# Storing an input-GEMM tile as one transfer of 576 KB instead of three of 192 KB

## What is computed

```python
def _layer(x, att_cache, ml_state, conv_buf, s5_state, p):
    h = _rmsnorm(x, g)
    (aq, ak, av, az, mq, mk, mv, mo, mz, mif, cb, cc, cx, cz, su, sz) = _split(h @ w_in)
    ya = band_attention(aq, ak, av, rel_bias)            # own chunk and 8 before it
    ym = sigmoid(mo) * mlstm(mq, mk, mv, mif, ml_state)
    yc = cb * conv3(cc * cx)
    ys = s5(su, ...)                                      # state space, GELU, GLU
    y = concatenate([silu(z) * yb for yb, z in ((ya, az), (ym, mz), (yc, cz), (ys, sz))])
    return x + y @ w_out
```

## Time and profile before

| | us |
|---|---|
| median of 3 runs | 2525.08 |
| lowest and highest of them | 2524.63, 2527.05 |
| the profiled execution | 2520.97 |
| its span, first to last instruction | 2519.2 |
| TensorE's mean granted clock in it | 0.969 of full |

### The profile page before, as it was taken

The page is one execution under the profiler, slowest core; times in us unless marked ns, Lnnn a source line. Parts: engine busy times, 40 slices in busy tenths (PEclk is TensorE's granted clock), DMA queues, the critical chain, the costliest instruction groups (busy, mean ns, idle before and its releaser), DMA issues.

```text
span 2519.2 us, 36324 instructions
## 1 busy us (share of the span) xinstructions
PE 2375.7 (94%) x14397; PEld 2179.6 (87%) x14397; DVE 753.8 (30%) x1225; ACT 479.5 (19%) x794; POOL 504.5 (20%) x292
## 2 busy tenths in 40 slices
PE   5999999999999999899999999999999765999997
PEld 4999999989999999899998898989999544888886
DVE  7220000022222221111163643531122355353433
ACT  6110000112222222122201011010110102343321
POOL 1222222222222222122222221212121340000000
PEclk8999999999999999999999999999999877999999
DMA  5121212432323231333232221322232648455562
GB/s 200 54 70 61 71 60 78 147 110 102 120 95 126 89 132 65 131 122 119 105 106 81 81 89 57 114 90 68 95 99 82 211 145 299 139 194 199 192 221 83
DMA packets 149949, 296.13 MB, mean 118 GB/s; under 512 B 26080, under 2 KB 89036, under 8 KB 146016
## 3 DMA queue, kind: packets, MB, share of 16 engines
q1 hardware_dynamic: 141792, 278.54, 32.4%
q10 hardware_dynamic: 8064, 16.25, 1.9%
HBM read 234.91 MB, written 78.70 MB: 124 GB/s over the span
## 4 chain that ended last, share of the span: by engine, by line
PE 86%; DVE 6%; DMA 5%; issue 1%; SPq 1%; ACT 1%; DVEq 0%; ACTq 0%; POOLq 0%
PE G L801 20%; PE G L803 19%; PE G L802 19%; PE X L1131 3%; PE X L1132 3%; PE X L1133 3%; PE G L1131 2%; PE G L1132 2%; PE G L1133 2%; PE X L1004 1%; PE X L983 1%; PE X L893 1%; PE X L886 1%; PE X L855 1%; PE X L998 1%
## 5 line engine op out<-in xcount | busy, mean ns | idle before, releaser
L801 PE MATMUL G<-hhi,whi 128*128 128x384 f32 x2928 | 1006.7, 344 | 8.1 <-issue 6.2
L802 PE MATMUL G<-hlo,whi 128*128 128x384 f32 x2928 | 985.2, 336 | 0.0
L803 PE MATMUL G<-hhi,wlo 128*128 128x384 f32 x2928 | 985.2, 336 | 0.0
L801 PEld LDWEIGHTS G<-hhi,whi 128*128 128x128 f32 x2928 | 554.2, 189 | 34.1 <-issue 24.6
L802 PEld LDWEIGHTS G<-hlo,whi 128*128 128x128 f32 x2928 | 554.6, 189 | 1.1
L803 PEld LDWEIGHTS G<-hhi,wlo 128*128 128x128 f32 x2928 | 553.7, 189 | 0.0
L773 POOL CAST whi<-wr 128x1024 fp32r<-128x1024 f32 x122 | 137.2, 1125 | 1473.9 <-PE G L803 1338.4
L775 POOL TENSOR_TENSOR wlo<-wr,whi 128x1024 fp32r<-128x1024 f32 x122 | 307.3, 2519 | 9.8
L1148 ACT ACTIVATE ev<-G 128x384 f32<-128x384 f32 x183 | 89.7, 490 | 871.6 <-PE G L803 871.3
L1852 DVE TENSOR_TENSOR olo<-orw,ohi 128x1024 fp32r<-128x1024 f32 x96 | 112.2, 1221 | 176.0 <-ACT ohi L1344 175.8
L1344 ACT ACTIVATE ohi<-orw 128x1024 fp32r<-128x1024 f32 x96 | 95.4, 1050 | 203.5 <-DMA orw<-w_out_t 74.3
(11 more groups left out here) (366 smaller groups left out, 2024.4 us busy)
## 6 DMA issues: line engine op xcount, KB each, us to landing
wr<-w_in_t SPq DMA_DIRECT2D x122, 512.0 KB, 4.5
orw<-w_out_t SPq DMA_DIRECT2D x96, 512.0 KB, 5.0
u_scratch<-ev SPq DMA_DIRECT2D x183, 192.0 KB, 1.9
xin<-x_all SPq DMA_DIRECT2D x9, 1024.0 KB, 4.8
cv<-u_scratch SPq DMA_DIRECT2D x16, 576.0 KB, 7.5
yr<-y_scratch SPq DMA_DIRECT2D x12, 768.0 KB, 9.0
xo<-x_all SPq DMA_DIRECT2D x3, 3072.0 KB, 12.4
y_all<-fo SPq DMA_DIRECT2D x9, 1024.0 KB, 4.0
```

Source lines behind the costliest of these rows:

```text
L801: mm(G[:, j, 0:GC], whi[:, kh, k], hhi[:, kk, hs], start=(kk == 0), stop=False)
L802: mm(G[:, j, 0:GC], whi[:, kh, k], hlo[:, kk, hs], start=False, stop=False)
L803: last = mm(G[:, j, 0:GC], wlo[:, kh, k], hhi[:, kk, hs], start=False, stop=(kk == 15))
```

## The change

The three stores of a tile become one. `store_u` is called once for a tile, where the store of bank 2 was; it waits for the evacuation of bank 2 (the count 3T + 6 covers all three banks) and sends the whole row of 1152 columns, 4608 B for each partition, where a bank's row had 1536 B. The three semaphores `u_stored[j]` become one. ScalarE's evacuation of any bank of tile T waits until the whole tile T - 1 has landed, where it waited for its own bank alone; `stored` waits once in place of three times. Bytes, buffers and the order on the engines are otherwise the same.

```diff
-        u_stored = [sem(f"u_stored{j}") for j in range(3)]
+        u_stored = sem("u_stored")
...
-            def store_u(T, j):
-
-                sp.wait_ge(evac_done, 3 * T + j + 4)
-                sp.dma_start(uT[T, :, GC * j:GC * j + GC], ev[:, j]).then_inc(u_stored[j], 16)
+            def store_u(T):
+
+                sp.wait_ge(evac_done, 3 * T + 6)
+                sp.dma_start(uT[T], ev[:, :, :].rearrange("p j n -> p (j n)")).then_inc(u_stored, 16)
 
             def gemm(T, kh, j, more=True):
                 if j == 0 and more:
                     load_w(T + 1, kh)
-                if kh == 1:
-                    store_u(T, j)
+                if kh == 1 and j == 2:
+                    store_u(T)
 
             def stored(T):
 
-                for j in range(3):
-                    sp.wait_ge(u_stored[j], 16 * T + 32)
+                sp.wait_ge(u_stored, 16 * T + 32)
...
             def evac(T, kh, j, func, scale=1.0):
                 if kh == 1:
                     act.wait_ge(bank_full, 3 * T + j + 4)
-                    act.wait_ge(u_stored[j], 16 * T + 16)
+                    act.wait_ge(u_stored, 16 * T + 16)
```

More of the change, by code:

```diff
@@ L730, in _ @@
             for s, n in ((xt_mm, 16), (h_done, 4), (w_split, 2), (half0_mm, 1), (bank_full, 3), (evac_done, 3),
-                         (u_stored[0], 16), (u_stored[1], 16), (u_stored[2], 16), (s_mm, 1), (s_add, 1),
+                         (u_stored, 16), (s_mm, 1), (s_add, 1),
                          (tp_mm, 1), (tp_evac, 1), (y_done, 1), (ay_stored, 16), (kt_mm, 4), (so_mm, 3), (sy_done, 1),
```

## The result

The median of six runs of the kernel after is 2534.02 us (2530.70 to 2537.69), against 2523.99 us for six runs of the kernel before: 1.0039 times the time, 95% interval 1.0028 to 1.0050. The change costs some 10 us; the forecast was 2528.0 us, from 2523.5 to 2532.0. A second set of runs of the same two kernels gave 1.0029 (1.0018 to 1.0039), some 7 us. So the direction that the sum had was right (+2.9 us), the size was less than half of what was measured, and "within 0.2%", which had most of the chances, was wrong.

The account below looks back on a forecast made before the run. The prediction took TensorE's matmuls as the bound (busy 94% of the span); removed issues were worth 0, and stage-end delays of 0.93 + 0.93 + 0.15 + 0.93, some 2.9 us, on a 2525.08 us median gave 2528.0 us, range 2523.5 to 2532.0.

Parts of the forecast that it names:

- A: Stage end at 486 us, tile 16: last store, K and V copies and `az` load all start later; +0.93 us, bounds 0 to 0.95.
- Rival 4: Whole kernel: 122 fewer transfers save their fixed parts; under 2520.0 us; chance 0.03 for faster by over 5 us.
- Rival 1: Hidden: the engines make good the burst at A, B and D; 0 to 1.5 us, some 2525.8 us; chance 0.24.
- B: Stage end at 1002 us, tile 32: `az` store queued behind the last store delays the sample stage's loads; +0.93 us.
- D: Stage end at 1687 us, tile 52: GELU and S5 state stores land later, delaying the first mLSTM load; +0.93 us.
- C: Stage end at 1260 us, tile 40: gaps between four `sz` stores absorb most extra bytes; +0.15 us, bounds 0 to 0.93.
- E: Stage end at 1965 us, tile 60: room for the extra bytes, so `gl` load starts unchanged; 0, bounds 0 to 0.93.
- rival 3: Behind C: longer TensorE idle time drops its clock to half, costing 1.5 to 3 us; some 2530.5 us; chance 0.12.
- Rival 2: Ends of S5 groups 0 to 2: burst delays TensorE's instruction loads, 3 x 0.93 = 2.8 us more; 2530.8 us; chance 0.08.

Follow-up runs that it names:

- e4_after_pad16: The kernel after with 16 small transfers added to SP's queue in the dense stage, ahead of the convolution's first state store; 1.0022 times the kernel before.
- e5_before_table_late: The kernel before with one redundant VectorE memset in each S5 group, so that VectorE's power table is made later; 1.0029 times the kernel before.

## Why the prediction was wrong

**The frame held.** TensorE is the bound, the dense stage kept its pace, the 122 removed issues are worth nothing (0.9992 with 56 tiles merged), a 576 KB store took 2.73 us at A where 2.78 was read for it, and TensorE was busy all of the 350 us of the dense stage, so it waited for no evacuation. Rival 4, faster by the fixed part of each transfer, is ruled out. The Trainium skill, DMA: Bandwidth & Descriptors, section Anatomy of one DMA — SWDGE (gpsimd) path, has a fixed cost of some 2.0 us a transfer; the estimate made from it, 244 us for 122 transfers one after the other, shows nowhere in the runs. Rival 1, hidden, is ruled out at B and D, and at A on the mean.

**B and D were right.** Over all twenty traces B's idle time is 8.69 to 8.98 us (nine) with tile 32 in three stores and 9.61 to 10.72 (eleven) with it in one, 1.2 more on the mean; D's is 2.13 to 2.82 us (nine) with tile 52 in three stores and 3.15 to 3.51 (eleven) with it in one, 0.9 more. The forecast was 0.93 for each.

**Three terms failed: A was too small, and what C and E set off was put at nothing.** No one of them carries the miss: the runs have 1.6 to 3.5 us at A in place of 0.93, 1.3 behind C in place of 0, and some 1.5 behind E in place of 0.

**A: "the two queues share to the end, and a later start of one stays a later end".** I priced the delay of SP's eight copies and of `az` at its own length, 0.93, and gave it 0.95 as its upper bound. The rows show that the copies that start later also lose share, and that SP takes 0.8 us longer to issue them. A's idle time over the traces that can be compared (ScalarE's issue at 0.8 us, copies in their place, no hold):

| tile 16 leaves in | idle time at A, us | mean |
|---|---|---|
| three stores | 6.02, 8.33, 9.43, 6.53, 6.55, 6.86 | 7.3 |
| one store | 10.22, 9.95, 8.37, 7.71, 9.08, 8.10, 8.64 | 8.9 |

That is 1.6 us on the mean (by the scatter in the two rows between 0.1 and 3.0, so the table alone would not rule out 0.93); the single-end runs, on one chip, gave 3.5 us of time for 2.9 of idle time. I put it between 1.6 and 3.5, against 0.93 with a bound at 0.95. The row that should have warned me was on the table: `az` took 17.60 us for 512 KB, where the stretch at B moves 428 GB/s, so its time was made by its neighbours and not by its bytes.

**C: "passes on what there is"; rival 3 had the right place with the wrong start.** The idle time itself went from 2.08 to 2.46 us on the mean of ten traces each, 0.38 where I had 0.15. What I didn't see is what hangs on it: VectorE's table, half a microsecond ahead of GpSimd's cast. Four executions in ten pay 3.1 to 3.5 us for that, 1.3 on the average over them. Rival 3 priced a fall of the clock behind C at 1.5 to 3 us and blamed the idle time at C; the clock there stayed full even behind 2.86 us of idle time (`e4_after_pad16`, 1.00 from 1282 to 1297 us), and fell behind the new wait of 1.49 us. (My reading of the bytes at C was loose too: the slices from 1258.95 to 1259.85 have a mean of 290 GB/s, which is not full beside 428.)

**E: "finds the store landed".** The load of `gl`, which I had looked at, cost nothing that can be told from scatter: its first matmul comes 22.3 to 24.0 us behind the last projection tile with tile 60 in three stores, 23.2 to 23.9 in the five traces of after. (The 0.34 MB that I read there are 0.30 by the row; that changes nothing.) But the stretch behind tile 60 is longer with one store on every chip that has both kinds, 1.5 us on the average, where I had 0, and in the first pair of traces 4.8 of the 5.9 us arise between 2010 and 2070 us of before, where the convolution begins, behind the loads with which my reading of E ended.

**Rival 2.** The wait for instructions at the first group end was 2.24 us before and 2.16 after; a second pair of traces had 2.10 and 2.45. There is no 0.93 per end.

**The sum, as it should have been:** A 1.6 to 3.5, B 1.2, C 0.4 and 1.3, D 0.9, the tail 1.5, together 6.9 to 8.8 us, against 10.0 and 7.3 us measured in two sets of runs. Without A the sum is 5.3, and the two kernels with later copies differ by 5.7 (4.3 by the ratios). The parts of the tail and of A are averages over traces that scatter by more than their size, and how a store at tile 60 delays the convolution is open.

The range failed for one reason: I had bounded each stage's cost by the bytes' own time, and added nothing for what meets what in the stages behind. The chance of 0.17 for "slower by over 0.2%" was put on rivals at two places, while the sum of four delays already stood at 2.9 of the 5 us that were needed. That the direction came out right is owed to B and D above all, where the mechanism held.

## What to carry to other kernels

Merging transfers could have paid only where someone waits for their fixed part, and here nobody does; where they end a stage, the last bytes leave later, and the stage end pays for them. A delay is worth its own length only if nothing else starts at that moment: where another queue's large copies or another engine's operation begin within a microsecond, ask which comes first now and what it costs to come second. Take a second trace of the kernel before, too: two of them differed by 7.7 us, more than twice the forecast. Here the copies on ScalarE's queue were worth as much as the change: issued later, they made the kernel before 8 us faster by the ratio (0.9967) and 10 by the medians.

## What the runs showed of the hardware

- A 512 KB load took 7.9 and 8.6 us with the other queue empty and 16.3 to 21.3 beside two copies of 1984 KB on it. How the two queues share depends on which starts first: with eight 320 KB copies on SP's queue starting 0.9 us later, the first 1984 KB copy on ScalarE's queue landed in 12.4 to 14.3 us in place of 15.4 to 17.1, and the eight copies in 12.8 to 13.2 (median of eight) in place of 11.2 to 12.0 (seven traces against six).
- A VectorE operation of 0.42 us (128x256, two inputs) that starts behind a GpSimd operation took 1.15 to 2.51 us and ended 0.28 or 0.29 us after it (`after` and `e5_before_table_late`, two operations each).
- The issue of the first 1984 KB copy took ScalarE's queue 0.79 to 0.81 us in sixteen traces and 2.47 to 2.70 us in the four of kernels whose evacuations have one wait more. What makes the difference was not tried.
- An 8 KB store landed 7.3 to 11.0 us after its issue in one and the same stage, by the kernel and by the execution.
